# The third and fourth sum of each full chunk change places between an accumulating DMA and VectorE

## What is computed

```python
D_MODEL = 2048
SEQ = 256
D_FF = 5632
def swiglu(x, wg, wu, wd):
    return (jax.nn.silu(x @ wg) * (x @ wu)) @ wd
...
        h = layer_norm(DN_ALPHA * h + 0.5 * swiglu(h, ffn1_wg[l], ffn1_wu[l], ffn1_wd[l]), ln1_g[l], ln1_b[l])
        mix = token_mixer(h, w_in[l], conv_dw[l], conv_db[l], conv_ln_g[l], conv_ln_b[l],
                          w_conv_out[l], w_attn_out[l], w_out[l])
        h = layer_norm(DN_ALPHA * h + mix, ln2_g[l], ln2_b[l])
        h = layer_norm(DN_ALPHA * h + 0.5 * swiglu(h, ffn2_wg[l], ffn2_wu[l], ffn2_wd[l]), ln3_g[l], ln3_b[l])
```

## Time and profile before

| | us |
|---|---|
| median of three runs | 2176.12 |
| the profiled execution | 2173.46 |
| its span (first to last instruction) | 2171.7 |
| PE busy | 2136.9 |
| DVE busy | 1734.4 |
| ACT busy | 1310.4 |
| DMA made by POOL's queue, share of 16 engines | 15.4% |
| DMA made by SP's queue, share of 16 engines | 54.0% |

### The profile page before, as it was taken

One profiled execution on the slowest core, in us unless ns is written; L12 is line 12 of the kernel. 1 busy time (PEld: TensorE's weight loads), 2 busy tenths in 40 slices (PEclk: granted clock), 3 DMA queues, 4 the chain that ended last, 5 costly groups with the idle time before them and its releaser, 6 DMA issues.

```text
span 2171.7 us, 25619 instructions
## 1 busy us (share of the span) xinstructions
PE 2136.9 (98%) x9556; PEld 1771.3 (82%) x9556; DVE 1734.4 (80%) x1438; ACT 1310.4 (60%) x1303; POOL 169.9 (8%) x281
## 2 busy tenths in 40 slices
PE   8999999999999999999999999998999999999997
PEld 6888888888887888888888888886888888888886
DVE  7799999999977567677776465658899999999986
ACT  5677777777752544454545344434677777777761
POOL 0111111111010000000000000000111111101110
PEclk9999999999999999999999999999999999999999
DMA  8688888888764555555455555555678888898862
GB/s 349 233 289 273 272 268 282 264 284 298 259 242 146 203 205 172 173 185 186 153 173 192 193 196 188 217 204 203 232 233 272 269 269 293 289 301 276 291 249 85
DMA packets 97372, 508.17 MB, mean 234 GB/s; under 512 B 13440, under 2 KB 13824, under 8 KB 56704
## 3 DMA queue, kind: packets, MB, share of 16 engines
q1 hardware_dynamic: 81216, 433.50, 54.0%
q0 software_dynamic: 16064, 73.42, 15.4%
HBM read 493.23 MB, written 13.63 MB: 233 GB/s over the span
## 4 chain that ended last, share of the span: by engine, by line
PE 95%; DVE 2%; DMA 1%; ACT 0%; issue 0%; SPq 0%; POOL 0%; DVEq 0%; ACTq 0%
PE acc L1635 11%; PE acc L1634 11%; PE acc L1633 11%; PE acc L1696 11%; PE acc L1698 11%; PE acc L1697 11%; PE tb L1698 9%; PE tb L1697 9%; PE tb L1696 9%; PE tb L1681 1%; DMA g_raw<-in_groups 1%; DVE g_lo L1030 1%; DVE act_sb L1296 0%; DMA raw<-in_stream 0%; PE tb L1957 0%; PE tb L1971 0%
## 5 line engine op out<-in xcount | busy, mean ns | idle before, releaser
L1030 DVE TENSOR_TENSOR g_lo<-g_raw,g_hi 128x2048 fp32r<-128x2048 f32 x370 | 837.9, 2284 | 120.9 <-ACT g_hi L637 120.3
L637 ACT ACTIVATE g_hi<-g_raw 128x2048 fp32r<-128x2048 f32 x370 | 706.5, 1916 | 263.1 <-PE acc L1698 82.8
L1007 DVE TENSOR_TENSOR w_lo<-raw,w_hi 128x1024 fp32r<-128x1024 f32 x272 | 326.9, 1220 | 170.7 <-ACT w_hi L597 167.3
L597 ACT ACTIVATE w_hi<-raw 128x1024 fp32r<-128x1024 f32 x272 | 279.0, 1057 | 165.0 <-PE acc L1635 99.4
L1633 PE MATMUL acc<-w_hi,xT_hi 128*128 128x512 f32 x768 | 302.2, 393 | 0.0
L1635 PE MATMUL acc<-w_hi,xT_lo 128*128 128x512 f32 x768 | 299.4, 390 | 0.0
L1634 PE MATMUL acc<-w_lo,xT_hi 128*128 128x512 f32 x768 | 299.2, 390 | 0.0
L1696 PE MATMUL acc<-g_hi,xF_hi 128*128 128x512 f32 x696 | 273.3, 393 | 15.4 <-DVE g_lo L1383 9.1
L1697 PE MATMUL acc<-g_lo,xF_hi 128*128 128x512 f32 x696 | 272.0, 391 | 0.0
L1698 PE MATMUL acc<-g_hi,xF_lo 128*128 128x512 f32 x696 | 272.0, 391 | 0.0
L1696 PE MATMUL tb<-g_hi,xF_hi 128*128 128x512 f32 x568 | 221.0, 389 | 0.0
(11 more groups left out here) (148 smaller groups left out, 2866.1 us busy)
## 6 DMA issues: line engine op xcount, KB each, us to landing
g_raw<-in_groups SPq DMA_DIRECT2D x262, 1024.0 KB, 7.0
raw<-in_stream SPq DMA_DIRECT2D x272, 512.0 KB, 4.4
g_raw<-in_groups POOLq DMA_DIRECT2D x48, 1024.0 KB, 8.0
bounce<-h_sq POOLq DMA_DIRECT2D x44, 256.0 KB, 4.9
h_in<-bounce POOLq DMA_DIRECT2D x176, 64.0 KB, 2.7
ln_gb<-in_ln SPq DMA_DIRECT2D x6, 1024.0 KB, 5.3
g_raw<-in_groups SPq DMA_DIRECT2D x4, 512.0 KB, 7.6
res<-in_x_rows SPq DMA_DIRECT2D x1, 2048.0 KB, 16.4
```

Source lines behind the costliest of these rows:

```text
L597: act.activation(w_hi[:, seg.split(j)], raw[:, seg.raw(j)], ACT.Copy).then_inc(hi_ready, 1)
L637: act.activation(g_hi[:, n % RING], source[:], ACT.Copy).then_inc(g_hi_ready, 1)
L1007: dve.tensor_tensor(w_lo[:, s], raw[:, seg.raw(j)], f32(w_hi[:, s]), ALU.subtract).then_inc(lo_ready, 1)
L1030: dve.tensor_tensor(g_lo[:, n % RING], source[:], f32(g_hi[:, n % RING]), ALU.subtract).then_inc(g_lo_ready, 1)
```

## The change

Two halves change places. T3a (`ra` plus `ua`) is made by an accumulating DMA in place of DVE; T4a (`qa` plus `ga`) by DVE in place of the DMA. The number of sums of each kind stays as it was, five and three in a full chunk.

- On DVE, T3a stood between the lo parts of D2 and P5a. T4a now stands behind T4b, ahead of P4a's lo part.
- On POOL, T4a's DMA was the last of a chunk's round. T3a's DMA now stands right behind T1b's, ahead of the round trip of the hidden values; it waits for T1a, which reads `ra`.
- ACT's split of P7a waits for `t3a_ready`, that of P4a for `t_ready`.

```diff
-FULL_SUMS = ("T1a", "T3a", "T2a", "T2b", "T4b")
+FULL_SUMS = ("T1a", "T2a", "T2b", "T4b", "T4a")
...
-                split_sum(f, b, "P7a", "ra", "T3a")
+                act.wait_ge(t3a_ready, fulls(f, b))
+                split(f, b, "P7a", "ra")
...
-                act.wait_ge(t4a_ready, fulls(f, b))
-                split(f, b, "P4a", "qa")
+                split_sum(f, b, "P4a", "qa", "T4a")
...
-                load_done(f, b, "ua")
-                dve.wait_ge(t_ready, G.sum_no[f, b, "T1a"])
-                add(ra, ra, ua)
                 lo_group(f, b, "P5a", "qa")
                 split_done(f, b, "P5a")
+                load_done(f, b, "ua")
                 add(qa, qa, ua)
...
                 add(qb, qb, gb)
+                load_done(f, b, "ga")
+                split_done(f, b, "P6a")
+                add(qa, qa, ga)
                 lo_group(f, b, "P4a", "qa")
...
                         add_from_hbm(f, b + 1, "qb", "rb", t1b_ready)
+                        pool.wait_ge(t_ready, G.sum_no[f, b + 1, "T1a"])
+                        add_from_hbm(f, b + 1, "ra", "ua", t3a_ready)
                     hidden_out(f, b)
                     hidden_in(f, b)
...
                         add_from_hbm(f, b + 1, "rb", "ub", t3b_ready)
-                        pool.wait_ge(g_lo_ready, lo_count(G.at[f, b + 1, "P6a"]))
-                        add_from_hbm(f, b + 1, "qa", "ga", t4a_ready)
```

More of the change, by code:

```diff
@@ L345, in build @@
         t3b_ready = sem("t3b_ready")
-        t4a_ready = sem("t4a_ready")
+        t3a_ready = sem("t3a_ready")
         seeded = sem("seeded")
@@ L1132, in full_block @@
             def full_block(f, b):
-                qa, qb, ra, ua, ub, gb = (source(f, b, name) for name in ("qa", "qb", "ra", "ua", "ub", "gb"))
+                qa, qb, ra, ua, ub, ga, gb = (source(f, b, name) for name in ("qa", "qb", "ra", "ua", "ub", "ga", "gb"))
                 lo_group(f, b, "P1a", "qa")
```

## The result

The changed kernel took 2230.29 us (median of four runs, 2225.21 to 2232.61); the kernel before, measured beside it, took 2176.03 (median of four, 2175.85 to 2177.44). The ratio is 1.0248, with a 95% interval of 1.0235 to 1.0261: 54 us slower, where 32 had been forecast.

The account below looks back on a forecast made before the run. PE was taken as the bound, never idle in full chunks; stalls of 1.48 (T4a on DVE) plus 0.5 us (T3a in POOL's queue) times 16 chunks add 31.7 us, giving 2208 us, range 2184 to 2255.

Parts of the forecast that it names:

- the forecast proper: Full chunks: a mean stall of 1 to 3.2 us each, 2192 to 2227 us in all, chance 0.55.
- What bounds the kernel: Full chunks: PE is busy for all 59.84 us, so a change of sums can only add idle time.
- T3a off DVE is worth nothing: DVE: 2.2 us freed at T3a gain nothing, since ACT's splits from P3a on wait for PE.
- T4a on DVE, 4.26 us later, 1.48 us a chunk: Before P4a: its lo part comes 4.26 us later against a mean lead of 2.82, so PE stalls 1.48 us.
- small stall: Rival at P4a: D3 or the bounce comes earlier, a chunk loses 0.3 to 1 us, 2181 to 2192; chance 0.15.
- T3a in the queue, 0.5 us a chunk: POOL's queue: T3a's DMA delays bounce and T3b, making D3, T4b, T4a and P4a 0.5 us later still.
- How the two terms add: Full chunks: 1.48 plus 0.5 gives 1.98 us a chunk, times 16 is 31.7 us.
- P7b hidden, 1 us left: P7b: lo part ends at about 201.2, PE wants it at 202.25, so T3b's later landing is hidden there.
- The signs: Profile after: PE stands once a chunk, before P4a, about 2 us; wrong if at P7b or D3, or clock falls.
- The round trip as the bound: Rival: bounce 4.8 behind T3a, T3b lands at 200.0, P4a 5.0 us late, 2256; chance 0.20 with or without clock.
- The clock: Rival: half clock after PE waits, 10 to 14 us from three or four chunks, at worst 2310; within the 0.20.
- The estimate by the Trainium skill's page: POOL's DMAs: 4.4 us for 1 MB would make the 0.5 vanish, leaving 16 x 1.48 = 24 us.

Follow-up runs that it names:

- the second experiment: Changed kernel with T4a left out altogether, T3a still by DMA ahead of the bounce: 2175.97 us, ratio 1.0007.
- first experiment: Kernel before with T4a moved to DVE, T3a kept on DVE, POOL's queue with T1b and T3b alone: 2184.22 us, ratio 1.0043.
- the third experiment: Changed kernel with ACT's save of P6b's bank moved ahead of the wait for T3b and P7b's split: 2238.39 us, ratio 1.0305.

## Why the prediction held its direction and missed the size

The time of 2230 lies above the 2192 to 2227 of the forecast proper, though inside the whole range. That the mean stall of 3.15 us still lies in its 1 to 3.2 is luck: of the two terms one was far too large and the other far too small.

- *What bounds the kernel*: right. No full chunk of any kernel here is shorter than 59.84 us.
- *T3a off DVE is worth nothing*: right. Without T3a and T4a on DVE (the second experiment) the time is that of before: DVE is busy for 1.9 us less in chunk 3, and no chunk is shorter.
- *T4a on DVE, 4.26 us later, 1.48 us a chunk*: the shift was right (chunk 2, with a lead of 4.20, lost 0.30 instead of 0.1, since PE's hand-over is 0.25 and not 0.04), the lead was not. The mean lead of 2.82 was read with D3's load slowed by T4a's DMA, which the change removes. Alone, the term is 0.33 (first experiment). This is the first mis-sized term, too large; the mechanism of the rival "small stall" was the truth for this half alone.
- *T3a in the queue, 0.5 us a chunk*: too small. The chain was right up to POOL: T1b at -1.6 (measured -1.7), T3a's DMA at 0.6 (0.4), T3b's at 22.2 (21.6). T3a landed 8.7 and not 7.0 behind T1b, and the two halves of the bounce at 16.7 and 18.7 in place of 14.9 for all of it; but T3b's DMA followed 2.9 us behind the later half, where my sum had 7.3 behind the earlier. Those 7.3 held a stop of 2.70 us in POOL, within the issue of the last `h_in`, which was 0.25 in the changed kernel. POOL before:

```profile
176.37 3.82 POOL L1596 DMA_DIRECT2D h_in<-bounce  x7 [4.22 <-DMA bounce<-h_sq]
182.89 0.55 POOL L1596 DMA_DIRECT2D h_in<-bounce  x1 [2.70 <-issue]
```

T3b took 9.3 in place of 7.9, so it landed at 30.9 in place of 30.06, and D3's split came at 33.2 in place of 32.5. Chunk 3 lost 2.83 against my 1.94: 0.7 from D3's split, the rest from the hand-over.
- *How the two terms add*: this is the step that failed in its reasoning. I priced them one by one. Without T4a the queue costs 0, without the queue T4a costs 0.33, and together the 14 chunks lose 49.8 us, 3.6 each. D3's split in the changed kernel is timed by T3b alone, so the loss has a threshold: up to a landing at 28.4 it is T4a's 0.33 alone, and above that landing - 28.1.
- *"P7b hidden, 1 us left"*: P7b's product was, but not the save behind its split, for which PE's P7a waits. In the full chunks PE stands at P7a once T3b lands later than about 30.1. It adds nothing while P4a is later still, as the table shows.
- *The spread*: at 2.83 each, 14 chunks would lose 39.6. The other 10 come nearly all from five chunks in which T3b took 10.4 to 13.3 us to land (2, 5 is the longest). Why some do is open: in chunk 5 of the second network D3's load, issued after it, landed before it (at 29.0). This spread was no term of the sum, and without it the changed kernel would have taken some 10 us less.
- *The signs*: PE was to stand once a chunk, at P4a. It stands at P7a as well, in 13 of the 14 chunks, and the clock falls inside three of them, which had been named as a sign of being wrong. The bounce did move and P4a was late, as forecast.
- *The round trip as the bound*: this rival came true in part. The bounce's later half landed 4.0 us behind T3a, near its 4.8, but T3b landed 2.2 us earlier than it had it (30.9 against 33.1).
- *The clock*: it fell inside three full chunks, after idle times at P7a of 2.3, 2.4 and 5.2 us. The length of one wait does not tell it: in the experiment with D4's lo part made twice a wait of 2.64 us at P7a (chunk 5) left the clock at 1.00. Nor does it fall only once a wait is over: in the kernel before it was half from 681.80 on the earlier trace rows, 1.1 us before the wait of 3.16 ended. As P4a would have been late anyway, it cost little: 8.00 against 7.5 in the worst chunk, and nothing beyond the formula in the chunks (1, 5) and (2, 4) of the table. The Trainium skill's page "TensorE: Matmul & The Clock Gate", section "HAM oscillation - how this bites in real kernels", describes the loop that waits once a turn and pays each time; the third experiment comes nearest to it, paying 1.6 us in ten of 16 chunks.
- *The estimate by the Trainium skill's page* "DMA: Bandwidth & Descriptors" (4.4 us for 1 MB): the traces disagree, with 7.7 to 9.3 us for an accumulating transfer in chunk 3, up to 13.3 in other chunks, and 8.7 between two in a row.
- *Outside the full chunks* I expected nothing, and 4.2 us came. Of these, 2.3 lie in the chunk behind the full ones of each network, 1.13 in each, where PE waits for a lo part. The same 1.13 stand there in the first experiment and in the one without T1b, 0.7 and 0.9 with T4a ahead of T4b, and nothing in the second experiment and in the one with both sums on DVE and T4a first. So these belong to T4a's place too. Of the other 1.9, 0.8 lie ahead of the first full chunk and the rest between the networks. The second experiment, whose full chunks take the time of before, came out 3.0 longer in the first of these stretches and 0.5 shorter in the other, so they can't be laid to the change.

## What to carry to other kernels

When a change takes the lead of one engine and lengthens a queue that this engine feeds, price the two together: follow the later start once around to the place where the lead was taken, and look for the time up to which each delay is hidden (here, T3b's landing at 28.4). A lead read from the trace before holds only while what limits it stays; here the transfer that the change removed had been eating it. Of two sums on one engine, make first the one for which another engine still has work to do: that alone was worth some 8 us between the two kernels with six sums on DVE (2184.22 and 2176.54).

## What the runs showed of the hardware

- A small transfer behind accumulating ones in POOL's queue waits for them: the bounce (256 KB) took 5.1 us where the transfer ahead of it had all but landed, and 12.0 to 13.5 behind two that were in flight.
- POOL itself can stand within an issue: 6.61 us in front of the sixth `h_in`, until 0.3 us after a transfer of 1 MB ahead of it had landed. In the kernel before it stood 2.70 us in front of the eighth with no sum's DMA in flight, so what ends such a stop is not shown.
- A lateness of PE of 2.3 to 2.9 us left the clock at 1.00 (2.4 GHz) in all eight chunks in which it came as two waits. In the third experiment, as one wait of 2.25 us or more, it was followed by 0.51 (1.2 GHz) for 3.4 us in ten chunks of 16 and by nothing in six. What decides between them is open.
